# Value projection of a two-block transformer kernel: token tiles outermost, and V taken out of PSUM bank by bank

## What is computed

```python
h = rmsnorm(x, g_norm1) * (1 + sc1) + sh1           # 256 latent tokens
hc = rmsnorm(ctx, g_norm1) * (1 + csc1) + csh1      # 256 context tokens
z = jnp.einsum('btd,dp->btp', h, w_in)              # the same for hc
gq, gk, gv, gg, glr, mq, mk, mv, mo, mgate = jnp.split(z, PROJ_SPLITS, axis=-1)
gla_v = gv.reshape(b, t, GLA_HEADS, GLA_DV).astype(f32)
ml_v = mv.reshape(b, t, MLSTM_HEADS, MLSTM_DV).astype(f32)
```

## Time and profile before

| | |
|---|---|
| median of 3 runs | 2794.07 us (2790.99 to 2797.41) |
| the profiled execution, its own time | 2803.37 us |
| span in the trace, first to last instruction | 2801.6 us |
| PE busy, share of the span | 2707.7 us, 97% |
| DVE busy | 2027.4 us, 72% |
| ACT busy | 1421.3 us, 51% |
| mean granted TensorE clock | 0.984 |
| DMA | 530.26 MB, mean 189 GB/s |
| values 0 to 15 in the trace | 249 to 459 us |

### The profile page before, as it was taken

How to read it: one execution, slowest core, us unless ns; L and a number is a source line. 1 busy time by engine, 2 the same in 40 slices (tenths; PEclk the granted TensorE clock), 3 DMA queues, 4 the chain that set the end, 5 groups by cost and what they waited for, 6 DMA issues and landing times.

```text
span 2801.6 us, 42126 instructions
## 1 busy us (share of the span) xinstructions
PE 2707.7 (97%) x15974; PEld 2345.6 (84%) x15974; DVE 2027.4 (72%) x3086; ACT 1421.3 (51%) x2000; POOL 0.2 (0%) x4
## 2 busy tenths in 40 slices
PE   7899999999999999999999999999999999999999
PEld 3568778988888888888888888889988998988887
DVE  6686786984898888886555777777655798556577
ACT  6443433444455555554444655554444654575564
POOL 0000000000000000000000000000000000000000
PEclk9999999999999999999999999999999999999999
DMA  8666666550654554545555455545555444432444
GB/s 340 230 256 268 239 242 239 203 211 31 255 178 182 183 192 180 190 184 178 190 188 189 157 189 185 180 175 182 186 182 193 161 174 165 178 142 106 169 153 148
DMA packets 108297, 530.26 MB, mean 189 GB/s; under 512 B 8288, under 2 KB 8832, under 8 KB 56336
## 3 DMA queue, kind: packets, MB, share of 16 engines
q1 hardware_dynamic: 105648, 515.93, 50.9%
q10 hardware_dynamic: 2528, 12.66, 1.2%
HBM read 526.46 MB, written 2.10 MB: 189 GB/s over the span
## 4 chain that ended last, share of the span: by engine, by line
PE 63%; DVE 9%; issue 3%; ACT 3%; ACTq 0%; DVEq 0%
PE ps L2025 33%; PE ps L2026 17%; DVE lo L1130 3%; PE ps L2017 3%; PE ps L2018 3%; PE ps L2019 3%; ACT hi L521 1%; PE ps L2362 1%; DVE ws L1721 1%; PE ps L2566 1%; PE ps L2564 0%; PE ps L2367 0%; DVE R L1768 0%; DVE O L1766 0%; DVE R L1807 0%
## 5 line engine op out<-in xcount | busy, mean ns | idle before, releaser
L1130 DVE TENSOR_TENSOR lo<-raw,hi 128x1024 fp32r<-128x1024 f32 x700 | 842.4, 1222 | 461.0 <-ACT hi L521 457.4
L521 ACT ACTIVATE hi<-raw 128x1024 fp32r<-128x1024 f32 x700 | 730.4, 1056 | 599.4 <-PE ps L2026 542.6
L2025 PE MATMUL ps<-x,hi 128*128 128x512 f32 x1376 | 488.7, 400 | 2.2 <-DVE x L1584 2.2
L2026 PE MATMUL ps<-x,lo 128*128 128x256 f32 x1376 | 387.5, 282 | 0.0
L2025 PE MATMUL ps<-xp,hi 128*128 128x512 f32 x1024 | 365.5, 402 | 4.4 <-DVE lo L1130 2.7
L2025 PE MATMUL ps<-y,hi 128*128 128x512 f32 x1024 | 364.6, 401 | 3.6 <-DVE y L1995 3.6
L2025 PEld LDWEIGHTS ps<-x,hi 128*128 128x128 f32 x1376 | 259.6, 189 | 67.6 <-issue 2.0
L545 ACT ACTIVATE hi<-raw 128x1024 fp32r<-128x1024 f32 x162 | 167.3, 1054 | 276.2 <-PE ps L2019 114.2
L2026 PE MATMUL ps<-xp,lo 128*128 128x256 f32 x1024 | 288.7, 282 | 0.0
L2026 PE MATMUL ps<-y,lo 128*128 128x256 f32 x1024 | 288.7, 282 | 0.0
L1193 DVE TENSOR_TENSOR lo<-raw,hi 128x1024 fp32r<-128x1024 f32 x162 | 192.5, 1220 | 101.2 <-ACT hi L545 100.9
(11 more groups left out here) (385 smaller groups left out, 5011.6 us busy)
## 6 DMA issues: line engine op xcount, KB each, us to landing
raw<-in_weights SPq DMA_DIRECT2D x483, 1024.0 KB, 4.8
wlast<-in_weights ACTq DMA_DIRECT2D x8, 1024.0 KB, 4.8
xf<-in_xt SPq DMA_DIRECT2D x8, 512.0 KB, 9.6
raw<-in_weights SPq DMA_DIRECT2D x4, 768.0 KB, 4.3
R<-in_xt ACTq DMA_DIRECT2D x1, 2048.0 KB, 7.3
out<-R SPq DMA_DIRECT2D x1, 1024.0 KB, 8.7
maskn<-in_maskn ACTq DMA_DIRECT2D x1, 512.0 KB, 3.6
ptr<-in_pt ACTq DMA_DIRECT2D x2, 256.0 KB, 3.8
```

Of the source, the lines that this page charges most:

```text
L521: act.activation(HI[p % PAIR][:, c], RAW[p % RING][:, c], ACT.Copy).then_inc(hi_ready, 1)
L1130: dve.tensor_tensor(LO[p % PAIR][:, c], RAW[p % RING][:, c], HI[p % PAIR][:, c].bitcast(F32), ALU.subtract).then_inc(lo_ready, 1)
L2025: pe.matmul(o, h, pair[:, :, k, :], start=start, stop=False, **kw)
L2026: return pe.matmul(o[:, 0, :], l, pair[:, 0, k, :], start=False, stop=stop, **kw)
```

## The change

Three edits belong together.

- **Order of the products.** A new function `value_half` takes the place of the inner function for values. In each half the four token tiles are outermost and the two blocks within, so PE writes six matmuls into PS[0], then six into PS[1], and so on. The number and the operands of the matmuls stay as they are.
- **Copies to V.** In the last half of a group each of PS[0], PS[1] and PS[2] is complete when its own six matmuls are through; PE signals that (`value_made`). ACT waits for it and copies the bank, ahead of its next split. Only PS[3] is still copied after `halves_used`, behind that split.
- **Waits of PE.** In the first half of values 4, 8 and 12 PE waits, ahead of each tile, for the copy of that tile's bank alone. Query 4 waits for 13 copies in place of 16.

```diff
@@ -544,6 +544,11 @@
                     act.wait_ge(halves_used, n - 3)
                 act.activation(half_of(HI, n), RAW[t % RING][:, h * SLOT // 2:(h + 1) * SLOT // 2], ACT.Copy).then_inc(hi_ready, 1)
 
+            def value_out(k, tt):
+
+                c = tt * 2048 + k // 4 * 512
+                act.activation(V[:, c:c + 512], PS[tt][:, :], ACT.Copy).then_inc(sem("value_evac"), 1)
+
             kview = K[:, :].rearrange("p (s b t) -> p s b t", s=2, b=8)
             NL = len(LEVELS)
 
@@ -580,6 +585,10 @@
                     act.activation(mrows[:, :], PS[6 + r % 2][0:16, :], ACT.Copy).then_inc(sem("mod_rows"), 1)
                 if (kind, k, half) == ("key4", 2, 1):
                     operand_hi(3)
+                if kind == "value" and k % 4 == 3 and half:
+                    for tt in range(3):
+                        act.wait_ge(sem("value_made"), 3 * (k // 4) + tt + 1)
+                        value_out(k, tt)
                 if UNITS[u] in HALF:
                     for m in ahead_of(u):
                         front_split(m)
@@ -610,9 +619,7 @@
                                    scale=DK ** -0.5 if k < 4 else 1.0).then_inc(sem("query_evac"), 1)
                 if kind == "value" and k % 4 == 3:
                     act.wait_ge(halves_used, HALF[UNITS[u]] + 1)
-                    for tt in range(4):
-                        act.activation(V[:, tt * 2048 + (k // 4) * 512:tt * 2048 + (k // 4 + 1) * 512], PS[tt][:, :],
-                                       ACT.Copy).then_inc(sem("value_evac"), 1)
+                    value_out(k, 3)
 
                 for m in range(4):
                     if n == AT["value", 2 * m] + 1:
@@ -2089,6 +2096,23 @@
                     ins = product(UNITS[u][2] * count // 2 + n, half_of(HI, m)[:, c], half_of(LO, m)[:, c])
                 ins.then_inc(halves_used, 1)
 
+            def value_half(u, k, half):
+
+                m = HALF[UNITS[u]]
+                pe.wait_ge(lo_ready, m + 1)
+                for tt in range(4):
+                    if k and k % 4 == 0 and half == 0:
+                        pe.wait_ge(sem("value_evac"), k - 3 + tt)
+                    for n in range(2):
+                        kk = 4 * (k % 4) + 2 * half + n
+                        w = slice(512 * n, 512 * n + 512)
+                        col = (tt // 2 * KD + kk) * T + tt % 2 * P
+                        ins = mm3(PS[tt][:, :], half_of(HI, m)[:, w], half_of(LO, m)[:, w], xh[:, col:col + P], xl[:, col:col + P],
+                                  kk == 0, kk == 15, swap=True)
+                    if k % 4 == 3 and half and tt < 3:
+                        ins.then_inc(sem("value_made"), 1)
+                ins.then_inc(halves_used, 1)
+
             def mod_slot(t, u):
 
                 r, g = mod_round(u)
@@ -2260,22 +2284,13 @@
                     elif k < 4:
                         pe.wait_ge(sem("query_evac"), k - 1)
                     else:
-                        pe.wait_ge(sem("value_evac"), 16)
+                        pe.wait_ge(sem("value_evac"), 13 if k == 4 else 16)
                         pe.wait_ge(sem("query_evac"), k - 1 if k >= 6 else 4)
                     half_slot(t, lambda n, h, l: one_stream((4 if k < 4 else 0) + k % 2, n, h, l))
                 if kind == "value":
                     if k == 0:
                         pe.wait_ge(sem("key_evac"), 8)
-                    if k and k % 4 == 0:
-                        pe.wait_ge(sem("value_evac"), k)
-
-                    def product(n, h, l):
-                        for tt in range(4):
-                            kk, s = 4 * (k % 4) + n, tt // 2
-                            c = slice((s * KD + kk) * T + (tt % 2) * P, (s * KD + kk) * T + (tt % 2 + 1) * P)
-                            ins = mm3(PS[tt][:, :], h, l, xh[:, c], xl[:, c], kk == 0, kk == 15, swap=True)
-                        return ins
-                    half_slot(t, product, 4)
+                    value_half(t, k, half)
                 if kind == "gate":
                     pe.wait_ge(sem("query_evac"), 7 + min(k, 1))
                     if k >= 2:
```

## The result

| | before | after |
|---|---|---|
| median of 6 runs each, one after the other on one chip | 2792.53 us (2785.56 to 2797.41) | 2775.20 us (2769.31 to 2783.28) |
| ratio, 95% interval | | 0.9924 [0.9897, 0.9952] |
| profiled execution, its own time | 2803.37 us | 2772.93 us |
| span in the trace | 2801.6 us | 2771.1 us |
| granted clock, mean | 0.984 | 0.988 |

Set against the 2794.07 us from which I forecast, the ratio gives 2772.8 us: 7.8 us under my 2780.6 and just under the low end of the range, 2773.0. The interval reaches from 2765.3 to 2780.7 us, so the forecast lies at its edge and the range's low end well inside it; the two medians alone give 0.9938, or 2776.7 us. The sign was right; the size of the measured gain was not. The questions for the experiments are whether the mechanism gives more than 13.5 us, and if not, where the rest comes from.

The account below looks back on a forecast made before the run. PE, busy 97% of the span, was taken as the bound, so gains must come from its pauses or clock. Groups 1 to 4 gave 2.4 + 5.0 + 1.6 + 4.5 = 13.5 us: 2794.1 to 2780.6 us, range 2773 to 2788.5.

Parts of the forecast that it names:

- the mechanism: At the four value groups' ends, copies to V run under matmuls, so PE's pauses and some clock falls go: 13.5 us.
- the steps: Lead expected by value 4, value 8, value 12, query 4 and first level argument: 2.4, 5.7, 9.0, 12.3, 13.5 us.
- the copies hidden: At group ends, three copies lie under the last half, the fourth ends about 1.9 us after it; PE never waits.
- the order free: In the value halves, changing bank every six matmuls in place of three costs nothing: 0.23 us from start to start.
- the start of the gates moving with PE: DVE starts the scan gates 1.01 us after its own pause, released by PE, so that start moves with PE.
- group 3: Third value group's end: the 1.57 us wait for V goes, 1.78 us and the clock's fall stay; worth 1.6 us.
- my first rival: The clock's fall behind the third value group goes too: 15.2 us gained, 2778.9 us; chance 28%.
- kend's wait: At group 4's end, PE would wait 0.5 us for kend during query 4, leaving 4.5 of 5.0 us.
- Each fall: Slower clock behind the pauses of groups 2, 3 and 4: 1.72, 1.70 and 1.72 us of full-speed work lost.
- two falls of the clock: In the range's low end: later pauses may lose or gain a fall, 1.7 us each way, once or twice.
- some scatter of the median: In the whole time: allowance that, with two falls of the clock, took the range's low end from 2778.9 to 2773 us.

Follow-up runs that it names:

- a_again: The changed kernel, unchanged, run again: median 2783.53 us (12 runs), ratio 0.9961 to the kernel before.
- a_third: The changed kernel, unchanged, run and profiled a third time: median 2782.85 us (12 runs), ratio 0.9964 to the kernel before.
- b_again: The kernel before, unchanged, run again: median 2797.3 us (12 runs), ratio 1.0000 to the same code.
- order_only: Against the changed kernel: new order kept, but all four copies to V behind the half and PE waiting for all; 2798.74 us, ratio 1.0011 to before.
- banks_only: Against the changed kernel: old order with blocks outermost, early copies and waits per bank kept; 2783.37 us, ratio 0.9950 to before.
- q4_all: Against the changed kernel: query 4 waits for 16 copies in place of 13; 2790.11 us in its one run.
- down_pause: Against the changed kernel: two longer PE pauses put into the feed-forward's second product, by waiting for the present block's copies; 2798.73 us in one run.
- sums_late: Against the changed kernel: the third group's column sums formed one half later; 2785.96 us (11 runs), ratio 0.9943 to before.

## Why the prediction was right and wrong

**Right: the mechanism and every term of its sum.** The lead table has 2.5, 5.8, 9.2, 12.6 and 13.6 us where the steps gave 2.4, 5.7, 9.0, 12.3 and 13.5. The values themselves took 196.8 us (249.38 to 446.22, forecast 197). a_again, a_third and b_again repeat it: 230.1 and 230.1 against 243.9 us. The whole times agree. In the three sets of runs that have both kernels the means differ by 16.4, 11.9 and 12.1 us, and over all their executions before has 2794.4 us (76) and the changed kernel 2780.9 us (30): 13.5 us, with a standard error of 1.6. The runs of before on a fourth chip (16, mean 2799.4 us) have none of the changed kernel beside them and are left out.

**Right: the copies hidden, the order free, the start of the gates moving with PE.** Shown by after's waits, by order_only (no gain) and banks_only (all of it but a longer fall of the clock), and by DVE's 1.01 us pause ahead of the first dec, which stayed.

**Right for the most part: group 3.** The 1.8 us for mods stayed and so did the fall of the clock, in after, a_again, a_third, q4_all and banks_only. In down_pause, the same code up to there, the fall came at 363, before PE's wait for mods, and the lead was 15.2 us (243.7 - 228.5): the number of my first rival, though not by its mechanism, a shorter pause. Whether the fall comes early or late was not forecast, and sums_late shows that taking the wait for mods away pays nothing. The Trainium skill ("TensorE: Matmul & The Clock Gate", section "What's actually happening") states that the moment of a transition varies from run to run. The traces agree, and go further in that the place varies too: in b_again, the same code as before, the clock fell behind group 1 (mean 0.66 in 303.5 to 307.5) and not behind group 2 (1.00 in 357.3 to 365.3), the reverse of the earlier trace rows, and the sum was the same to 0.2 us.

**Small misses.** kend's wait was 0.28 us, not 0.5. Each fall cost the 1.7 us taken for it in after, but twice that, 3.4 us, in banks_only and order_only; I had no row for a fall of that length.

**Wrong: the range, and in it one term, "some scatter of the median".** I let the low end be 2778.9 less two falls of the clock, 2775.5, and left 2.5 us for the scatter, to 2773; the measured 2772.8 lies 0.2 us under it. Runs of identical code spread over 29 us (before, 2781.3 to 2810.6; on one chip alone 26 us), more than half of them in two clusters, about 2785 to 2789 and 2798 to 2805 us. At least one cause of that is the feed-forward's two paces, 718.3 or 731.9 us in the same code, 13.6 us apart. The changed kernel's three profiled executions follow it: 2772.93 and 2774.01 us with the short stretch (after, a_third), 2786.77 with the long one (a_again). The profiled execution of before had the long one and stood 9.3 us above the median of three runs, which was to be read as a warning: I wrote the difference down and still left 2.5 us. The 6 runs of the first result then caught the changed kernel mostly on its better side: its median was 17.3 us lower, where 12 more runs give 10.2 us (a_again) and 12 more again 8.6 us (a_third). The pooled means differ by 13.5 us, as much as the sum forecast. So the size of the measured step beyond 13.5 us is scatter between executions, and the range should have allowed for it. With 6 runs of each kernel, on which side of 2773 the result came out was luck.

**Open.** What draws the pace of 391 or 398 ns; it changed across a pause of PE in down_pause and without one in b_again. Whether the kernel's code makes one pace likelier is not shown either: before has two profiles, both with the long stretch. Nor is it shown that the two clusters of the times are only that pace, since the stages of an execution are known from its profile alone.

## What to carry to other kernels

Where PE needs the banks that another engine has still to empty, look at the last block of the accumulation: each bank is complete at its own last matmul, and all but the last can be emptied under the others' matmuls, if the signals and the waits are per bank. Price a pause as its own length plus what the granted clock shows as lost behind it, and count the lead at each stage border, not in the total. Before a forecast or a verdict of half a per cent, compare stages that the change does not touch in the two profiles: here such a stage differed by as much as the change was worth.

## What the runs showed of the hardware

- The same 512-column matmul at granted clock 1.00 had a median of 391 or 398 ns in the feed-forward (394 in order_only): 718.3 or 731.9 us for the same 2064 pairs. The length changed across a pause of PE of 5.5 us (down_pause, at 1474.7) and also without a pause (b_again, at 2017).
- The granted clock can fall without a pause: in sums_late to 0.55 from 364, with PE busy for the whole of the 4 us before, and in down_pause to 0.57 from 363.4. Behind that lay eight one-column sums (361.05, 0.95 us, in sums_late) and 32-row matmuls; the same work in after (from 358.75) was followed by no fall.
- A pause of 2.4 us at the same place (group 1) left the clock at 1.00 in before and was followed by 0.66 in b_again, the same code.
- A fall of the clock cost 1.7 us in before and after, and 3.4 us behind group 3 in banks_only.
